# The constants' first columns and the first norm's weight in transfers of their own, and the position tables' products and the first high part moved ahead of the first turn

## The reference

```python
def _rms_norm(x, g):
    xf = x.astype(jnp.float32)
    y = xf * lax.rsqrt(jnp.mean(xf * xf, axis=-1, keepdims=True) + EPS)
    return (y * g.astype(jnp.float32)).astype(x.dtype)

def _swiglu(x, w_gate, w_up, w_down):
    return (jax.nn.silu(x @ w_gate) * (x @ w_up)) @ w_down
...
        hf = _swiglu(_rms_norm(x, g[0]), ffn_w_gate[layer, 0], ffn_w_up[layer, 0], ffn_w_down[layer, 0])
        x = x + 0.5 * _rms_norm(hf, g[1])
```

## Time and profile before

| | |
|---|---|
| median of 3 runs | 2291.13 us (2288.84 to 2291.92) |
| the profiled execution, own time | 2288.96 us |
| its span, first to last instruction | 2287.2 us |
| mean granted TensorE clock | 0.946 |
| busy: PE, DVE, ACT, POOL | 92%, 59%, 50%, 19% of the span |
| HBM traffic | 485.53 MB read, 12.10 MB written, 218 GB/s |

### The profile page before, as it was taken

The page is one execution under the profiler, slowest core; times in us unless marked ns, Lnnn a source line. Parts: engine busy times, 40 slices in busy tenths (PEclk is TensorE's granted clock), DMA queues, the critical chain, the costliest instruction groups (busy, mean ns, idle before and its releaser), DMA issues.

```text
span 2287.2 us, 31360 instructions
## 1 busy us (share of the span) xinstructions
PE 2098.6 (92%) x13218; PEld 1826.9 (80%) x13218; DVE 1351.0 (59%) x1302; ACT 1133.3 (50%) x1455; POOL 443.4 (19%) x305
## 2 busy tenths in 40 slices
PE   7998977999899899699999877999998986999997
PEld 6898967999899898699988666777777875877775
DVE  5766436556656584655653656566665247565665
ACT  4765445565566354456533534554443244454553
POOL 2683000474176100037510000000000000000000
PEclk9999988999999899799999988999998787999999
DMA  9897514787688463378754105878886203688874
GB/s 326 289 313 234 173 56 146 241 284 242 219 287 277 148 172 124 117 245 279 260 172 151 52 11 201 295 284 323 330 303 211 88 1 147 239 314 313 322 291 177
DMA packets 224348, 494.95 MB, mean 216 GB/s; under 512 B 11848, under 2 KB 167608, under 8 KB 199472
## 3 DMA queue, kind: packets, MB, share of 16 engines
q1 hardware_dynamic: 200608, 410.20, 52.3%
q0 software_dynamic: 23328, 81.71, 10.5%
q10 hardware_dynamic: 272, 1.05, 0.1%
HBM read 485.53 MB, written 12.10 MB: 218 GB/s over the span
## 4 chain that ended last, share of the span: by engine, by line
PE 82%; DVE 9%; ACT 3%; DMA 3%; issue 2%; POOL 0%; DVEq 0%; SPq 0%; ACTq 0%
PE psum L997 80%; DVE nrm L2069 2%; DMA big<-in_ada_w 2%; DVE low L2069 1%; DMA ring<-in_ffn_w_up 1%; PE psum L1063 1%; PE psum L1596 1%; ACT wh L1685 1%; PE psum L1240 1%; DVE xl L2069 1%; DVE wide L2069 0%; DMA ring<-in_moe_w_gate 0%; DVE nrm L2189 0%; DVE x L2392 0%; DVE nrm L2163 0%
## 5 line engine op out<-in xcount | busy, mean ns | idle before, releaser
L2069 DVE TENSOR_TENSOR low<-ring,wh 128x2048 fp32r<-128x2048 f32 (+2 forms) x338 | 811.3, 2416 | 532.0 <-ACT wh L1685 530.7
L1685 ACT ACTIVATE wh<-ring 128x2048 fp32r<-128x2048 f32 (+2 forms) x338 | 640.6, 1902 | 436.9 <-PE psum L997 236.8
L997 PE MATMUL psum<-xh,wh 128*128 128x256 f32 x1832 | 520.7, 284 | 13.4 <-DVE xl L2069 7.2
L997 PE MATMUL psum<-xl,wh 128*128 128x256 f32 x1832 | 520.0, 284 | 0.0
L997 PE MATMUL psum<-xh,low 128*128 128x256 f32 x1832 | 517.7, 283 | 0.0
L997 PEld LDWEIGHTS psum<-xh,wh 128*128 128x128 f32 x1832 | 352.1, 192 | 19.2 <-issue 15.5
L997 PEld LDWEIGHTS psum<-xl,wh 128*128 128x128 f32 x1832 | 350.1, 191 | 1.4
L997 PEld LDWEIGHTS psum<-xh,low 128*128 128x128 f32 x1832 | 350.5, 191 | 0.0
L769 POOL TENSOR_TENSOR big<-big 128x1024 f32<-128x1024 f32 x144 | 302.7, 2102 | 241.3 <-ACT big L1781 233.3
L997 PE MATMUL psum<-wh,xh 128*128 128x256 f32 (+5 forms) x864 | 278.6, 322 | 10.4 <-DVEq L667 5.9
L997 PE MATMUL psum<-wh,xl 128*128 128x256 f32 (+5 forms) x864 | 277.7, 321 | 0.0
(11 more groups left out here) (350 smaller groups left out, 2389.3 us busy)
## 6 DMA issues: line engine op xcount, KB each, us to landing
ring<-in_moe_w_gate SPq DMA_DIRECT2D x64, 1024.0 KB, 5.4
ring<-in_moe_w_up SPq DMA_DIRECT2D x64, 1024.0 KB, 6.0
ring<-in_moe_w_down SPq DMA_DIRECT2D x64, 1024.0 KB, 5.4
big<-in_ada_w POOLq DMA_DIRECT2D x48, 1024.0 KB, 6.7
ring<-in_ffn_w_gate SPq DMA_DIRECT2D x44, 1024.0 KB, 6.2
ring<-in_ffn_w_up SPq DMA_DIRECT2D x44, 1024.0 KB, 5.9
ring<-in_ffn_w_down SPq DMA_DIRECT2D x44, 1024.0 KB, 5.2
ring<-in_mlstm_w_in SPq DMA_DIRECT2D x16, 1024.0 KB, 5.6
```

The costliest lines, as they stand in the source:

```text
L997: return pe.matmul(out_, lhsT, rhs, start=start, stop=stop, **kw)
L1685: act.activation(wh[n % PARTS][:, 0:w], ring[SLOT_OF[n]][:, 0:w], ACT.Copy).then_inc(high, 1)
L2069: return dve.tensor_tensor(out_, a, b, op)
```

## The change

- The constants' columns are reordered: the identity, and the two epsilons behind it, come first (130 columns), so that SP's transfer takes these only. The other 1944 columns are loaded by ScalarE's queue, with a semaphore of their own, for which TensorE, ScalarE and VectorE wait at the first ffn stage.
- Gain 0 is loaded by ScalarE's queue too, ahead of those columns, and no longer by POOL. Its semaphore is its own, and the count of buffer 0 is one lower from then on.
- TensorE's part of setup becomes `tables()`, called at the beginning of the first turn, ahead of the transposes. The first turn uses banks 4 to 7.
- ScalarE's high part of gate 0 moves from setup to the end of the first norm, ahead of the four copies of the turn.

```diff
--- before.py
+++ after.py
@@ -80,7 +80,9 @@
 
 
 C_IDENT = 0
-C_MSTRICT = C_IDENT + P
+C_EPS = C_IDENT + P
+C_EPS4 = C_EPS + 1
+C_MSTRICT = C_EPS4 + 1
 C_STICK = C_MSTRICT + P
 C_MINCL = C_STICK + W3
 C_CAUSAL = C_MINCL + W3
@@ -89,11 +91,9 @@
 C_COS = C_ONES + P
 C_SIN = C_COS + TT * 32
 C_LOWER = C_SIN + TT * 32
-C_EPS = C_LOWER + 16
-C_FLIP = C_EPS + 1
+C_FLIP = C_LOWER + 16
 C_IOTA = C_FLIP + P
-C_EPS4 = C_IOTA + P
-C_BLOCK = C_EPS4 + 1
+C_BLOCK = C_IOTA + P
 NCONST = C_BLOCK + H
 
 
@@ -218,6 +218,8 @@
         act_step = sem("act_step")
         dve_step = sem("dve_step")
         const_in = sem("const_in")
+        const_rest_in = sem("const_rest_in")
+        first_gain_in = sem("first_gain_in")
         x_in = sem("x_in")
         gain_in = [sem(f"gain{i}_in") for i in range(GAINBUFS)]
         gain_used = sem("gain_used")
@@ -698,7 +700,7 @@
 
             n = 0
             sp.dma_start(x[:, :, :], I["x"][0].rearrange("(t p) d -> p t d", p=P)).then_inc(x_in, 16)
-            sp.dma_start(const[:, :], I["const"]).then_inc(const_in, 16)
+            sp.dma_start(const[:, 0:C_MSTRICT], I["const"][:, 0:C_MSTRICT]).then_inc(const_in, 16)
             for kind, what, more in stream:
                 if kind == "one":
                     load(n, what, more)
@@ -792,7 +794,6 @@
                             load_ada_bias(turn + 1)
                 pool.wait_ge(ada_out, 16 * (q0 + 3))
 
-            load_gain(0)
             small_in(aux[0:32, 0:8], I["rel_bias"])
             small_in(aux[0:32, 8:16], I["rel_table_2"])
             small_in(big[0:32, 0:R_END], I["rows"])
@@ -924,8 +925,16 @@
 
             return k * FC, 3 * k * FC
 
+        def turn_bank(k):
+
+            return 4 if k == 0 else 0
+
         def wait_gain(eng, g):
-            eng.wait_ge(gain_in[g % GAINBUFS], 16 * (g // GAINBUFS + 1))
+
+            if g == 0:
+                eng.wait_ge(first_gain_in, 16)
+            else:
+                eng.wait_ge(gain_in[g % GAINBUFS], 16 * (g // GAINBUFS + (g % GAINBUFS > 0)))
 
         GB, UB = 4, 6
         route = aux
@@ -1023,7 +1032,7 @@
             def x_half(s, half):
                 pe.wait_ge(turn_low, 4 * (ran(s, "turn") - 1) + 3 + half)
 
-            def setup(s, k):
+            def tables():
                 pe.wait_ge(extra_in, EXTRA["setup"])
                 pe.transpose(psum[:, 0, 0:8], aux[0:8, 16:144], ident[0:8, 0:8])
                 mm(psum[0:8, 1, 0:W3], aux[0:32, 0:8], big[0:32, 0:W3], True, True)
@@ -1048,6 +1057,8 @@
 
             def turn(s, k):
 
+                if k == 0:
+                    tables()
                 for q in range(4):
                     t, half = q // 2, q % 2
                     if JOINED[s] and half == 0:
@@ -1060,7 +1071,7 @@
                             last = mm(psum[:, q, i * P:(i + 1) * P], x[:, t, f:f + P],
                                       diagonal(s - 1, t), True, True)
                         else:
-                            last = pe.transpose(psum[:, q, i * P:(i + 1) * P], nrm[:, t, f:f + P], ident)
+                            last = pe.transpose(psum[:, turn_bank(k) + q, i * P:(i + 1) * P], nrm[:, t, f:f + P], ident)
                     last.then_inc(turned, 1)
 
             def route_products(turn_, t):
@@ -1656,11 +1667,13 @@
                 give_back(3)
                 give_back_last()
 
-            fns = {"setup": setup, "turn": turn, "ffn": ffn, "moe": moe, "project": project, "outproj": outproj,
+            fns = {"turn": turn, "ffn": ffn, "moe": moe, "project": project, "outproj": outproj,
                    "stick": stick, "soft": soft_attention, "mlstm": mlstm, "norm": norm,
                    "residual": residual, "latent": latent, "router": router}
             pe.wait_ge(const_in, 16)
             for s, (name, args, _) in enumerate(STAGES):
+                if name == "ffn" and INSTANCE[s] == 0:
+                    pe.wait_ge(const_rest_in, 16)
                 if name in fns:
                     fns[name](s, INSTANCE[s], *args)
                 boundary(pe, s + 1)
@@ -1691,7 +1704,8 @@
 
             def setup(s, k):
                 for j, shape in enumerate(early(s + 1)):
-                    high_part(PIECE0[s] + j, shape)
+                    if j:
+                        high_part(PIECE0[s] + j, shape)
                 act.wait_ge(setup_dve, 1)
                 act.activation(small[:, S_R:S_R + 8], small[:, S_R:S_R + 8], ACT.Silu).then_inc(setup_act, 1)
 
@@ -1708,6 +1722,8 @@
                         act.wait_ge(x_added, 2 * ran(s, "residual") - 2 + t + 1)
                     link(act.activation(sq[:, :], x[:, t, :], ACT.Square, accum_out=stat[:, t:t + 1]))
                     root_mean(stat[:, t:t + 1], D).then_inc(squared, 1)
+                if s == 0:
+                    high_part(PIECE0[2], GU)
 
             def turn_columns(s, k):
                 g = GAIN0[s - 1]
@@ -1733,7 +1749,7 @@
                     f = 4 * (q % 2)
                     act.wait_ge(turned, 4 * k + q + 1)
                     act.activation(xh[:, f:f + 4, (q // 2) * P:(q // 2 + 1) * P],
-                                   psum[:, q, :].rearrange("p (a b) -> p a b", a=4), ACT.Copy).then_inc(turn_high, 1)
+                                   psum[:, turn_bank(k) + q, :].rearrange("p (a b) -> p a b", a=4), ACT.Copy).then_inc(turn_high, 1)
                     if STAGES[s + 1][0] == "router" and q % 2:
                         token_rows(s, q // 2)
 
@@ -2039,8 +2055,13 @@
             fns = {"setup": setup, "norm": norm, "turn": turn, "ffn": ffn, "moe": moe, "project": project,
                    "outproj": outproj, "residual": residual, "stick": stick, "soft": soft_attention,
                    "mlstm": mlstm, "latent": latent, "router": router, "final": final}
+            act.dma_start(gain[0][:, :], GAINS[0].rearrange("(a n) -> a n", a=1).broadcast_to([P, D]))\
+                .then_inc(first_gain_in, 16)
+            act.dma_start(const[:, C_MSTRICT:NCONST], I["const"][:, C_MSTRICT:NCONST]).then_inc(const_rest_in, 16)
             act.wait_ge(const_in, 16)
             for s, (name, args, _) in enumerate(STAGES):
+                if name == "ffn" and INSTANCE[s] == 0:
+                    act.wait_ge(const_rest_in, 16)
                 if name in fns:
                     fns[name](s, INSTANCE[s], *args)
                 if name in ("ffn", "moe", "outproj"):
@@ -2211,7 +2232,7 @@
                     f = 4 * (q % 2)
                     place = (slice(0, P), slice(f, f + 4), slice((q // 2) * P, (q // 2 + 1) * P))
                     dve.wait_ge(turn_high, 4 * k + q + 1)
-                    tt(xl[place], psum[:, q, :].rearrange("p (a b) -> p a b", a=4), xh[place].bitcast(F32),
+                    tt(xl[place], psum[:, turn_bank(k) + q, :].rearrange("p (a b) -> p a b", a=4), xh[place].bitcast(F32),
                        ALU.subtract).then_inc(turn_low, 1)
 
             def low_part(s, n, shape):
@@ -2813,6 +2834,8 @@
             dve.wait_ge(const_in, 16)
             dve.wait_ge(x_in, 16)
             for s, (name, args, _) in enumerate(STAGES):
+                if name == "ffn" and INSTANCE[s] == 0:
+                    dve.wait_ge(const_rest_in, 16)
                 if name in fns:
                     fns[name](s, INSTANCE[s], *args)
                 boundary(dve, s + 1)
```

## The result

The change made the kernel slower: 2297.15 us (median of 20 runs, 2286.99 to 2305.61) against 2290.89 (median of 20). The ratio is 1.0029, interval 1.0017 to 1.0042, so +6.6 us, from 3.9 to 9.6. The forecast was 2292.0, within 2288.0 to 2295.3. The profiled execution took 2296.83 us, its span is 2295.0.

The account below looks back on a forecast made before the run. It took TensorE's inner matmul products as the bound, the beginning as a race of loads against the norm's chain. First product +2.7 and setup sums +0.9, partly absorbed by stops, left +0.9 on 2291.13: 2292.0 us, range 2288.0 to 2295.3.

Parts of the forecast that it names:

- The input's landing, up to 9.4: At the kernel's beginning: sharing turns with 1484 KB at 410 GB/s moves the input's landing from 5.80 by up to 3.6 us.
- The loads: Passage on the beginning's transfers: queues alternate by packet, 410 GB/s together, 203 in the small tables' stretch; landing moves up to 1.0 us.
- Gate 0's landing, 18.4 to 19.36: First gate weight piece lands at 18.4 if the tables hide beside large packets, 19.36 if not; middle taken, 18.9.
- The working's other case, 19.36: If spreading transfers over queues saves only issue time, gate 0's landing stays at 19.36 and the sum becomes +1.3.
- The high part in front of the turn: First norm on ScalarE: copies wait behind gate 0's high part, first product at 26.7 (+2.7), up piece's low part +0.9.
- Neither end costs anything: Tables' products ending by 17.3 and transposes by 21.3 cost nothing while ScalarE stands at gate 0's high part until 20.8.
- What is left of it: Behind the setup sums: TensorE's stops absorb its delay, and the later of two chains at 93.90 leaves +0.9 us.
- slower, by the late start of products: Rival: TensorE's slow-clock stretch behind the first product lasts twice as long after a pause; +3.9 us, 2295.0; chance 0.15.
- the norm moves earlier and matters: Rival: input undisturbed and gate 0 before 16 bring the first product before 24.01; 0 to -0.5 us, 2290.9; chance 0.1.
- both loads early: Rival: first gate and up pieces land early as the tables' slow stretch vanishes; -1.6 us, at most -3, 2288.1; chance 0.2.
- Chances: Odds for the whole kernel against about 0.2% (4.6 us): faster 0.07, same 0.85, slower 0.08.

Follow-up runs that it names:

- the tables held: The change, but POOL issues the 368 KB table and everything behind it only once the input has landed; ratio 1.0040.
- the constants' rest held: The change, but ScalarE issues the other 1944 columns of the constants only once the input has landed; ratio 1.0029.
- the new order: Kernel before, but SP loads the constants' other columns behind the first up piece, and POOL gains 1 to 3 inside the first ada_w turn; ratio 0.9982.
- the moves alone: Kernel before with tables' products ahead of the first turn (banks 4 to 7) and gate 0's high part ahead of the copies, transfers unchanged; ratio 1.0015.
- bias rows behind gate 0: The change, but POOL issues the bias rows only when TensorE has used gate 0, SP's event for the third gate piece; ratio 1.0005.
- the kernel before, held: Kernel before with five dummy copies on ScalarE ahead of its first high part, some 5.5 us; ratio 1.0026.

## Why the prediction was wrong

Its sign was right and its mechanism partly; the size was not: +0.9 forecast, +6.6 measured, and 2297.15 lies above the range.

- *The input's landing, up to 9.4.* **This is the first step that failed.** The working added 1484 KB of ScalarE's queue at 410 GB/s and left POOL's small tables out of it, though it had named the slow stretch (203 GB/s) itself, under "The loads". The input landed at 13.6. In the kernel before, the input and the constants (5.7 and 10.1) had landed when that stretch came, and gate 0 stood in it; the change put the input and the constants into it. With the tables held it landed at 10.1, with the constants' rest held at 11.5. The slower start, 87 instead of 142 GB/s in the first 4 us, is 0.22 MB, or by my estimate 0.5 us at 410 GB/s, and wasn't in the working either. The identity, which was to follow at once, came at 15.0, when the table load behind the input was done too, and the norm began at 15.00 instead of near 10.8. The last small table, put at 12.9 at the latest, came at 14.8.
- *Gate 0's landing, 18.4 to 19.36.* Mis-sized, and in the wrong direction: 21.27. The work ahead of gate 0 was the same, but the tables, instead of hiding beside large packets, slowed them for longer: 231 GB/s instead of 292 from 8 to 14 us. The working's other case, 19.36, was too early too. That the landing follows what is moved ahead of it held: 13.6 with the tables and gains issued behind the input, 13.7 in the new order.
- *The high part in front of the turn.* Right. From gate 0's landing to the first product the working has 7.8 us; the moves alone took 7.5 (19.63 to 27.15), the change 7.7 (21.27 to 28.94). What this chain was fed with was wrong: the setup sums, forecast 0.9 later, ended at 39.46 instead of 36.36, 3.1 later.
- *"Neither end costs anything" of the tables' products in front.* Right only under cover of the high part. Alone they cost 3.9 us.
- *What is left of it: the stops absorb, later of the two chains.* **This is the second step that failed.** I had the DMA's hole grow by up to 2.7 us, as one number, and no race in it. The third gate piece took 13.8 us instead of 5.6, the up piece behind it 22.9 instead of 14.2 and TensorE stopped for 4.68 at 70.02. Behind it, from 70 to 75, the granted clock was 0.50, the lower of the two levels:

```profile
60.00:65.00 5.00, 5.00 (x45) 5.00 (x44) 0.00 (x0) 0.00 (x0) 0.00 (x0) 1.00 1.03 356
...
70.00:75.00 5.00, 4.98 (x23) 4.99 (x24) 3.52 (x4) 3.75 (x3) 0.00 (x0) 0.50 0.89 275
```

  It made 23 matmuls there, 45 in the 5 us from 60. By these counts the lower level cost 5 x (1 - 23/45) = 2.4 us, an estimate, and the stops up to the landmark sum to 7.16 us instead of 4.48. Together that is 5.1, somewhat more than the 4.6 us that are new, and about half of it is idle time and half is clock. The kernel with the bias rows behind gate 0 shows that in the change this race is worth some 4 us of the first layer. How much of the total it is stays open: by that kernel's median most of it, by the kernel before, held, which lost as much without it, little.
- *Rival "slower, by the late start of products"*, 2295.0. Its direction was right and its price came nearest, but its reason was not what happened: the slow stretch behind the first product did not last twice as long (5.9 us before, 5.3 in the change). The late start alone, in the kernel before with ScalarE held, ends the layer 5.8 us late with a slow stretch of only 3.4.
- *Rival "the norm moves earlier and matters"*. The opposite happened: the norm began 4.9 us later (15.00 instead of 10.11), for the input was disturbed. In the new order, where it isn't, the norm begins at 7.24.
- *Rival "both loads early"* didn't occur in the change, but it did when the loads were put in that order: -2.9 at the first product and -3.05 at the landmark, where the rival had -3 as its far end.
- *Chances.* Slower by over 0.2% had 0.08. What was left out (the table beside the input, the race of two issues) could only cost, and the range should have been open on that side.

Shown by runs: the price of each half at the first product, the tables' share in the input's delay, the race. Argued only: that the difference of 1.5 us between TensorE's lateness and VectorE's comes from up 0's wait that vanished (read from the rows; no run changed it alone). Open: why the stretch with the 368 KB table, 32 rows of 11.8 KB, and the small tables is so slow, and how the total divides between late start and race.

## What to carry to other kernels

A transfer split off onto another queue takes turns with the one it was meant to relieve. Before splitting, list everything in flight in that stretch and ask which of it is needed first; the gain here came from sending 2.5 MB later, not from sending it on another queue. A step that waits for a load must not stand in an in-order engine ahead of work that is ready. And where a shift of a few microseconds is carried downstream, look for two issues on different engines that come within a microsecond of each other: at the end of the first layer, turning their order cost 1.6 to 5.0 us here, beside a shift of 3.9 to 5.2.

## What the runs showed of the hardware

- While the table of 368 KB into 32 partitions and the small tables behind it pass, everything beside them is slow: 238 GB/s at a DMA share of 1.05 with them (8 to 12 us of the change), 377 GB/s at 1.03 without them in the same window; where they were held, 16 to 18 us had 184. The Trainium skill (DMA: Bandwidth & Descriptors, Back-pressure in remote DMA) says of transfers between cores that stalled writes stall a source engine's other queues too. These loads are local ones, and no run here changed the table's shape, so whether that is the reason is not shown.
- A megabyte of 1 KB packets landed in 5.3 to 6.7 us when it was issued before, or up to 0.16 us behind, 4.7 MB of larger packets on another queue, in 10.1 at 0.45 us behind and in 13.2 to 16.2 from 0.82 us on. The piece issued behind it took 14.2 or 22.9 (the kernel before, the change).
- TensorE's clock fell behind some stops and not behind others of the same length. In the new order's trace a stop of 2.18 us ended at 70.02, and in 70 to 72 the granted clock was 1.00 and TensorE made 16 matmuls; another of 2.18 us ended at 89.40, and in 89.4 to 91.4 it was 0.50 and 9 matmuls. After 2.37 us at 97.13 (bias rows behind gate 0) the next product took 0.55, after 2.74 us at 75.34 in the kernel before 0.36.
